# Split weight slots lengthened by 16 bytes, and the tokens of the four stages moved, in a two-layer fp32 decoder trunk

## The chip, the cores and the metric

The kernel runs on one core of one Trainium2 chip. The metric is the device time of one execution in microseconds (us). Before the change it is 2213.77 us, the median of two runs (2213.63 and 2213.91 us).

## What is computed

Two decoder layers over 256 tokens of 2048 features, all in float32. Layer 0 mixes tokens with sliding-window attention (mixer A: 32 query heads, 4 key/value heads, a sink and a position bias); layer 1 with forgetting attention (mixer B: 32 heads of queries, keys and values, decay sums in the logits). After each mixer, and after each gated MLP (up to 2 x 5632, a causal convolution of width 3, SiLU gate, down to 2048), stands a scaled residual and a layer norm:

```python
def conv_ffn(x, w_up, conv_w, conv_b, w_down):
    h = conv(x @ w_up, conv_w) + conv_b          # 2048 -> 2*5632, width 3, causal
    g, u = h[..., :D_FF], h[..., D_FF:]
    return (jax.nn.silu(g) * u) @ w_down

for i in range(DEPTH):                            # DEPTH = 2
    y = swa_sink_attention(x, ...) if i % 2 == 0 else forgetting_attention(x, ...)
    x = layer_norm(ALPHA * x + y, ln_g[i, 0], ln_b[i, 0])
    y = conv_ffn(x, ffn_w_up[i], ffn_conv_w[i], ffn_conv_b[i], ffn_w_down[i])
    x = layer_norm(ALPHA * x + y, ln_g[i, 1], ln_b[i, 1])
```

## The kernel before, in words

All weights are streamed once through SBUF, in chunks of 256 x 512 values (512 KB). Chunk after chunk lands in one of four slots of `raw` (SyncE issues the transfers, line 299). ScalarE rounds the chunk to the reduced float32r form in `w_hi` (line 478), VectorE writes the remainder to `w_lo` (line 757). The tokens are kept in the same way, as `xh` and `xl`. A product of two float32 values is then three float32r matmuls: low weights by high tokens, high weights by low tokens, high by high. TensorE takes chunks from the slots in turn (slot = chunk number mod 4), so that the slot changes each time two k-tiles of 128 rows have been used. Its order is fixed by the program; waits are on counting semaphores.

There are two forms of product. What a form streams through the array is the moving operand, and what is loaded first by a separate weight load is the stationary one.

- *Turned* (`turned_product`, lines 1189, 1191, 1192, and `turned_first`, line 1204): 128 columns of the weights are stationary, 256 tokens are moving. Used for the queries of A (768 matmuls), queries and keys of B (1536), and both up-projections (4224 each, 22 column groups x 16 k-tiles x 4 x 3). 10,752 matmuls in all.
- *Not turned* (`product`, lines 1171 to 1173): 128 tokens are stationary, 512 columns of the weights are moving. Used for the keys and values of A (96), the values of B (384), the output projections (2 x 384) and the down-projections (2 x 1056). 3360 matmuls in all. In the output projections the stationary operand is `oh` or `ol`, in the down-projections `hid_h` or `hid_l`, elsewhere `xh` or `xl`.

Between the matmuls of the products, TensorE does the transposes and the small matmuls of attention (lines 1318 to 1345).

Where things lie within a partition of SBUF: `raw`, `w_hi`, `w_lo`, `xh`, `xl`, `oh`, `ol`, `hid_h` and `hid_l` begin at multiples of 256 bytes; the fillers `fill_to_res` and `fill_to_xh` see to that. A slot of `w_hi` or `w_lo` is 2 x 512 values, 4096 bytes, so each of the four slots begins at a multiple of 256 bytes too. The tokens of the four stages (mixer A, MLP of layer 0, mixer B, MLP of layer 1) lie in the same `xh` and `xl`, but each stage begins at its own place in them, `PLACES`, counted in values of 4 bytes: 192, 32, 128 and 64 bytes from the start. A k-tile of tokens is 1024 bytes, and the part of a weight row that one weight load takes is 512 bytes, so the place modulo 256 bytes is the same for all matmuls of a stage.

```python
PLACES = (48, 8, 32, 16)
PLACED = D // P * SEQ + 64
w_hi = sb("w_hi", [P, RING, 2, COLS], F32R)
w_lo = sb("w_lo", [P, RING, 2, COLS], F32R)
xhs, xls = ([t[:, at:at + KT * SEQ].rearrange("p (k t) -> p k t", t=SEQ) for at in PLACES] for t in (xh_all, xl_all))
```

Of the kernel before, what the change touches and what calls it, by code (L numbers as in the profile page):

```python
# [22 lines left out]
F32R = mybir.dt.float32r  # L23
# [3 lines left out]
P = 128  # L27
# [2 lines left out]
MT = SEQ // P  # L30


PLACES = (48, 8, 32, 16)
PLACED = D // P * SEQ + 64
DEPTH = 2
HD = 64
# [5 lines left out]
COLS = 512  # L42
# [4 lines left out]
UP_PAIRS = D_FF // COLS  # L47
OUT_GROUPS = D // COLS
RING = 4
AHEAD = 3  # L50
LOW_AHEAD = 2
ALPHA = (2 * DEPTH) ** 0.25
# [75 lines left out]
def trunk(nc, x, a_w_qkv, a_w_o, a_sinks, rel_bias, b_w_qkvf, b_f_bias, b_w_o,  # L128
          ffn_w_up, ffn_conv_w, ffn_conv_b, ffn_w_down, ln_g, ln_b, out):
    ctx = ExitStack()  # L130
    with ctx:
        def sb(name, shape, dt=FP32, where=ctx):
            return where.enter_context(nc.sbuf_tensor(name, shape, dt))

        def sem(name):
            return ctx.enter_context(nc.semaphore(name))
# [13 lines left out]
        sb("fill_to_res", [P, (1920 - 1592) // 4])  # L150
        res = sb("res", [P, MT, D])
        raw = sb("raw", [P, RING, 2, COLS])
        w_hi = sb("w_hi", [P, RING, 2, COLS], F32R)
        w_lo = sb("w_lo", [P, RING, 2, COLS], F32R)
        tok = sb("tok", [P, MT, COLS])
        cg = sb("cg", [P, 4, SEQ])
        cu = sb("cu", [P, 4, SEQ])
        lnp = sb("lnp", [P, 2, COLS])
        convcol = sb("convcol", [P, DEPTH, 4, 2 * FT])
        sb("fill_to_xh", [P, 320])  # L160
        with ExitStack() as first:
            xh_all = sb("xh", [P, PLACED], F32R, first)
        with ExitStack() as later:
# [28 lines left out]
        hid_l = sb("hid_l", [P, FT, SEQ], F32R)  # L192
        xhs, xls = ([t[:, at:at + KT * SEQ].rearrange("p (k t) -> p k t", t=SEQ) for at in PLACES] for t in (xh_all, xl_all))
        ps = ctx.enter_context(nc.psum_tensor("ps", [P, 8, COLS], FP32))
# [6 lines left out]

        raw_in = [sem(f"raw_in{i}") for i in range(RING)]
        res_in = [sem(f"res_in{i}") for i in range(4)]
# [87 lines left out]
        def _(sp):  # L291
# [4 lines left out]
            def load_chunk(w, col, b4, loc, c):  # L296
                if not (isinstance(b4, int) and 4 * b4 + loc < RING):
                    sp.wait_ge(low_ready, b4 * 4 + (loc - RING + 1))
                sp.dma_start(raw[:, loc % RING], w[:, 2 * c:2 * c + 2, bass.ds(col, COLS)]).then_inc(raw_in[loc % RING], 16)
# [161 lines left out]
        def _(act):  # L461
# [9 lines left out]
            def split(b4, loc):  # L471

                if isinstance(b4, int) and 4 * b4 + loc >= CH_END:
                    return
                act.wait_ge(raw_in[loc % RING], b4 * 16 + 16 * (loc // RING + 1))
                if not (isinstance(b4, int) and 4 * b4 + loc < RING):
                    act.wait_ge(chunks_used, b4 * 4 + (loc - RING + 1))
                act.activation(w_hi[:, loc % RING], raw[:, loc % RING], ACT.Copy).then_inc(high_ready, 1)  # L478

            def slots(b4, loc0, nk=KT):  # L480

                for k in range(nk):
                    if k == nk - 2:
                        split(b4, loc0 + k // 2 + AHEAD)
                    yield k
                    if k % 2 == 0 and k != nk - 2:
                        split(b4, loc0 + k // 2 + AHEAD)

            def split_run(b4, loc0, count):

                while loc0 % 4 and count:
                    split(b4, loc0)
                    loc0, count = loc0 + 1, count - 1
                if count >= 8:
                    with act.Fori(0, count // 4) as i:
                        for c in range(4):
                            split(i + (b4 + loc0 // 4), c)
                    loc0, count = loc0 + count // 4 * 4, count % 4
                for c in range(count):
                    split(b4, loc0 + c)  # L500

            def xt_evacuate(xi, l, s, g):

                xh = xhs[xi]
                if xi == 0:
                    act.wait_ge(xt_turned, g + 1)
                    src = ps[:, X_BANK + g % 4, :].rearrange("p (a t) -> p a t", a=2)
                else:
                    if g == 0:
                        act.wait_ge(first_turned, xi)  # L510
                        act.activation(xh[:, 0, :], ps[:, FIRST_BANK, 0:SEQ], ACT.Identity,
                                       scale=lncol[:, 0, l, s, 0:1], bias=lncol[:, 1, l, s, 0:1]).then_inc(first_high, 1)
                        act.wait_ge(xt_turned, KC * xi + 1)
                        act.activation(xh[:, 1, :], ps[:, X_BANK, SEQ:2 * SEQ], ACT.Identity,
                                       scale=lncol[:, 0, l, s, 1:2], bias=lncol[:, 1, l, s, 1:2]).then_inc(xt_high, 1)
                        return
                    src = cg[:, 2 * (g % 2):2 * (g % 2) + 2, :]
                    if g in DVE_FULL:
                        act.wait_ge(xt_full, FULLS * (xi - 1) + DVE_FULL.index(g) + 1)
                    else:  # L520

                        act.wait_ge(xt_low, KC * xi + g - 1)
                        act.wait_ge(xt_turned, KC * xi + g + 1)
                        for a in range(2):
                            k = 2 * g + a
                            last = act.activation(cg[:, 2 * (g % 2) + a, :], ps[:, X_BANK + g % 4, a * SEQ:(a + 1) * SEQ],
                                                  ACT.Identity, scale=lncol[:, 0, l, s, k:k + 1], bias=lncol[:, 1, l, s, k:k + 1])
                        own.link(last)
                act.activation(xh[:, 2 * g:2 * g + 2, :], src, ACT.Copy).then_inc(xt_high, 1)
# [58 lines left out]
            def norm_and_first(xi, l, s):  # L588

                layer_norm(xi)  # L590
                act.wait_ge(norm_ready, xi)
                for i in range(2):
                    normalise(i)
                xt_evacuate(xi, l, s, 0)
                for i in range(2, 6):
                    normalise(i)
                xt_evacuate(xi, l, s, 1)
                for i in range(6, KC):
                    normalise(i)
# [80 lines left out]
            def up_finish(k, l, n):  # L680

                if k in (1, 3):
                    conv(cu, 1, l, n, k - 1, hid_low, n + l * UP_PAIRS)
                if k == 9:
                    act.wait_ge(prod_ready, n + (l * UP_PAIRS + 1))
                    act.activation(hid_h[:, bass.ds(n * 4, 4), :], cu[:, :, :], ACT.Copy).then_inc(hid_high, 1)

            def mlp(l):
# [18 lines left out]
                for k in slots(b4, 0, KT):  # L707
                    up_finish(k, l, UP_PAIRS - 1)
                split_run(b4, KC + AHEAD, OUT_GROUPS * FC - KC - (AHEAD if l == DEPTH - 1 else 0))

# [3 lines left out]
            xt_evacuate(0, 0, 0, 1)  # L714
            for c in range(1, AHEAD):
                split(0, c)
# [11 lines left out]
            for l in range(DEPTH):  # L728
                if l == 1:
                    mixer_b()  # L730

                split_run(CH_O[l] // 4, 2 * KC + AHEAD, (OUT_GROUPS - 2) * KC)
                norm_and_first(1 + 2 * l, l, 0)
# [778 lines left out]
```

## Time and profile before

| | |
|---|---|
| median of the two runs | 2213.77 us |
| the profiled execution, its own time | 2213.89 us |
| its span, first to last instruction | 2212.1 us |
| mean granted TensorE clock | 0.996 of full speed |
| TensorE matmul busy | 2182.2 us, 99% |
| VectorE, ScalarE, GpSimd busy | 60%, 47%, 10% |

1.8 us of the profiled execution lie outside its span. Matmuls are pipelined: a matmul of 256 columns is shown with some 280 ns, though the next one starts 113 to 120 ns later. So the shown duration of a matmul is no measure of its cost; what counts is the distance between the starts of two matmuls that follow each other. In the stretches 340 to 740 us (MLP of layer 0, up), 800 to 1000 us (its down-projection), 1500 to 1900 us (MLP of layer 1, up) and 1980 to 2180 us (its down-projection) TensorE does nothing but products.

### The profile page before, as it was taken

What the parts mean: (1) busy time and instruction counts of PE and PEld (TensorE: products, weight loads), DVE (VectorE), ACT (ScalarE), POOL (GpSimd) and SP (SyncE); (2) the same over time, 40 slices, a digit from 0 to 9 for tenths busy, and PEclk for the clock granted to TensorE, in tenths of its full rate; (3) what the DMA queues carried; (4) which work ended last, traced back from release to release, by engine and by line L of the source; (5) the groups of instructions that cost most, each with busy time, mean ns of one, the idle gap of its engine ahead of it and who ended that gap; (6) DMA issues with size and microseconds to landing.
All of it is one profiled execution on the core that took longest, in us unless ns stands there. A gap on an engine that the chain in (4) does not pass through costs nothing.

```text
span 2212.1 us, 40894 instructions
## 1 busy us (share of the span) xinstructions
PE 2182.2 (99%) x15265; PEld 2033.5 (92%) x15265; DVE 1335.3 (60%) x1805; ACT 1039.1 (47%) x1380; POOL 217.7 (10%) x206
## 2 busy tenths in 40 slices
PE   9999999999999999999999999999999999999996
PEld 7998899999999988888899998899999999988885
DVE  5565676666666555446665565576666566654455
ACT  4554464554555443335444444364545454543332
POOL 2000002210000000000340330002230000000001
PEclk9999999999999999999999999999999999999998
DMA  8544557666666666565655654656666666665563
GB/s 266 153 154 154 179 172 206 196 198 188 189 185 187 188 192 194 193 192 156 199 173 170 190 175 139 205 157 198 196 202 185 187 185 185 188 226 194 192 194 108
DMA packets 206952, 408.71 MB, mean 185 GB/s; under 512 B 12652, under 2 KB 13756, under 8 KB 206620
## 3 DMA queue, kind: packets, MB, share of 16 engines
q1 hardware_dynamic: 200192, 385.92, 57.2%
q0 software_dynamic: 5776, 21.34, 3.0%
q8 instruction: 49, 0.80, 0.2%
q10 hardware_dynamic: 908, 0.43, 0.1%
q14 instruction: 27, 0.22, 0.0%
HBM read 405.46 MB, written 2.18 MB: 184 GB/s over the span
## 4 chain that ended last, share of the span: by engine, by line
PE 96%; DVE 3%; ACT 0%; DMA 0%; issue 0%; SPq 0%; ACTq 0%; DVEq 0%
PE ps L1192 19%; PE ps L1189 19%; PE ps L1191 19%; PE ps L1171 11%; PE ps L1173 11%; PE ps L1172 11%; PE ps L1319 1%; PE ps L1326 1%; PE ps L1338 1%; PE ps L1337 1%; PE ps L1318 1%; PE ps L1336 0%; DMA raw<-in_a_w_qkv_dram 0%; DVE cg L803 0%; PE ps L1345 0%; PE ps L1268 0%
## 5 line engine op out<-in xcount | busy, mean ns | idle before, releaser
L757 DVE TENSOR_TENSOR w_lo<-raw,w_hi 128x1024 fp32r<-128x1024 f32 x728 | 923.6, 1274 | 652.4 <-ACT w_hi L478 651.9
L478 ACT ACTIVATE w_hi<-raw 128x1024 fp32r<-128x1024 f32 x728 | 771.2, 1060 | 974.2 <-PE ps L1192 557.6
L1189 PE MATMUL ps<-xh,w_lo 128*128 128x256 f32 x3572 | 1007.2, 282 | 2.2 <-DVE xl L799 1.6
L1192 PE MATMUL ps<-xh,w_hi 128*128 128x256 f32 x3572 | 999.0, 280 | 0.0
L1191 PE MATMUL ps<-xl,w_hi 128*128 128x256 f32 x3572 | 997.4, 279 | 0.0
L1189 PEld LDWEIGHTS ps<-xh,w_lo 128*128 128x128 f32 x3572 | 670.7, 188 | 5.2 <-DVE xl L799 3.0
L1191 PEld LDWEIGHTS ps<-xl,w_hi 128*128 128x128 f32 x3572 | 672.0, 188 | 0.4
L1192 PEld LDWEIGHTS ps<-xh,w_hi 128*128 128x128 f32 x3572 | 671.4, 188 | 0.0
L1171 PE MATMUL ps<-w_lo,hid_h 128*128 128x512 f32 x704 | 273.9, 389 | 0.0
L1173 PE MATMUL ps<-w_hi,hid_h 128*128 128x512 f32 x704 | 273.9, 389 | 0.0
L1172 PE MATMUL ps<-w_hi,hid_l 128*128 128x512 f32 x704 | 273.9, 389 | 0.0
L1173 PEld LDWEIGHTS ps<-w_hi,hid_h 128*128 128x128 f32 x704 | 132.2, 188 | 27.4
L1171 PEld LDWEIGHTS ps<-w_lo,hid_h 128*128 128x128 f32 x704 | 132.2, 188 | 27.4
L1172 PEld LDWEIGHTS ps<-w_hi,hid_l 128*128 128x128 f32 x704 | 132.2, 188 | 27.4
L400 POOL COPY cw<-convcol 128x16 f32 (+1 forms) x40 | 39.8, 994 | 779.3 <-DVE cu L1087 431.5
L1171 PE MATMUL ps<-w_lo,oh 128*128 128x512 f32 x256 | 102.4, 400 | 0.0
L1173 PE MATMUL ps<-w_hi,oh 128*128 128x512 f32 x256 | 99.9, 390 | 0.0
L1172 PE MATMUL ps<-w_hi,ol 128*128 128x512 f32 x256 | 99.7, 390 | 0.0
L1087 DVE SCALAR_TENSOR_TENSOR cu<-ps,cw,cu 128x254 f32<-128x254 f32 (+1 forms) x176 | 76.5, 476 | 1.6
L1087 DVE SCALAR_TENSOR_TENSOR cg<-ps,cw,cg 128x254 f32<-128x254 f32 (+1 forms) x176 | 76.5, 476 | 1.6
L1171 PE MATMUL ps<-w_lo,xh 128*128 128x512 f32 x160 | 64.2, 401 | 3.1 <-issue 2.6
L1173 PE MATMUL ps<-w_hi,xh 128*128 128x512 f32 x160 | 63.6, 398 | 0.0
(164 smaller groups left out, 1499.3 us busy)
## 6 DMA issues: line engine op xcount, KB each, us to landing
raw<-in_ffn_w_up_dram SPq DMA_DIRECT2D x352, 512.0 KB, 3.6
raw<-in_ffn_w_down_dram SPq DMA_DIRECT2D x176, 512.0 KB, 4.7
raw<-in_b_w_qkvf_dram SPq DMA_DIRECT2D x96, 512.0 KB, 4.4
raw<-in_a_w_qkv_dram SPq DMA_DIRECT2D x40, 512.0 KB, 4.5
raw<-in_a_w_o_dram SPq DMA_DIRECT2D x32, 512.0 KB, 4.6
raw<-in_b_w_o_dram SPq DMA_DIRECT2D x32, 512.0 KB, 4.7
bias<-rel_by_distance POOLq DMA_DIRECT2D x4, 1024.0 KB, 6.5
bias<-minus_cumulated_decay POOLq DMA_DIRECT2D x4, 1024.0 KB, 6.5
```

The costliest lines, as they stand in the source:

```text
L400: gp.tensor_copy(cw[:, h], convcol[:, l, :, bass.ds(n * 4 + h * FT, 4)]).then_inc(cw_ready, 1)
L478: act.activation(w_hi[:, loc % RING], raw[:, loc % RING], ACT.Copy).then_inc(high_ready, 1)
L757: dve.tensor_tensor(w_lo[:, s], raw[:, s], w_hi[:, s].bitcast(FP32), ALU.subtract).then_inc(low_ready, 1)
L1087: last = dve.scalar_tensor_tensor(dst[:, j, lag:SEQ], src, cw[:, h, tap, j:j + 1], dst[:, j, lag:SEQ], ALU.mult, ALU.add)
L1171: pe.matmul(o, lh[:, k, rows], w_lo[:, slot, k % 2, :], start=(k == 0), stop=False)
L1172: pe.matmul(o, ll[:, k, rows], w_hi[:, slot, k % 2, :], start=False, stop=False)
L1173: last = pe.matmul(o, lh[:, k, rows], w_hi[:, slot, k % 2, :], start=False, stop=(k == nk - 1))
L1189: pe.matmul(o, w_lo[:, slot, k % 2, cols], xh[:, k, :], start=(k == 0 and j % 2 == 0), stop=False, skip_group_check=True)
L1191: pe.matmul(o, w_hi[:, slot, k % 2, cols], xl[:, k, :], start=False, stop=False, skip_group_check=True)
L1192: last = pe.matmul(o, w_hi[:, slot, k % 2, cols], xh[:, k, :], start=False, stop=(k == KT - 1), skip_group_check=True)
L1318: pe.matmul(o[:, 0:P], qT[:, s // 2, 0:P], kz[:, kt, s % 2, 0:P], start=True, stop=True)
L1319: pe.matmul(o[:, P:SPAN], qT[:, s // 2, P:SEQ], kz[:, kt, s % 2, :], start=True, stop=True).then_inc(scores_ready, 1)
```

## The change

Each slot of `w_hi` and `w_lo` gets 4 values (16 bytes) more, which nothing uses. Slots 0 to 3 then begin 0, 16, 32 and 48 bytes past a multiple of 64 bytes (slot 0 of each tensor at a multiple of 256). A new filler lets `w_lo` begin at a multiple of 256 bytes again, and a shorter `fill_to_xh` leaves `xh` and all after it where they were; `tok`, `cg`, `cu`, `lnp` and `convcol` in between lie 320 bytes later. The tokens of the four stages move to 240, 192, 112 and 64 bytes. `raw` stays as it is. The instructions of each engine, their order and their waits stay the same.

```diff
-PLACES = (48, 8, 32, 16)
+PLACES = (60, 48, 28, 16)
 PLACED = D // P * SEQ + 64
...
 RING = 4
+SLOT = 2 * COLS + 4
...
-        w_hi = sb("w_hi", [P, RING, 2, COLS], F32R)
-        w_lo = sb("w_lo", [P, RING, 2, COLS], F32R)
+        w_hi = sb("w_hi", [P, RING, SLOT], F32R)[:, :, 0:2 * COLS].rearrange("p s (a c) -> p s a c", a=2)
+        sb("fill_to_w_lo", [P, 48])
+        w_lo = sb("w_lo", [P, RING, SLOT], F32R)[:, :, 0:2 * COLS].rearrange("p s (a c) -> p s a c", a=2)
...
-        sb("fill_to_xh", [P, 320])
+        sb("fill_to_xh", [P, 240])
```

## Rows read from the trace of the kernel before

**Rows 1.** The page: span, busy time of each engine, and the chain that ended last.

```profile
span 2212.1 us, 40894 instructions
PE 2182.2 (99%) x15265; PEld 2033.5 (92%) x15265; DVE 1335.3 (60%) x1805; ACT 1039.1 (47%) x1380; POOL 217.7 (10%) x206
...
PE 96%; DVE 3%; ACT 0%; DMA 0%; issue 0%; SPq 0%; ACTq 0%; DVEq 0%
```

**Rows 2.** Groups of instructions: busy us, mean ns of one, then idle time before, releaser.

```profile
L757 DVE TENSOR_TENSOR w_lo<-raw,w_hi 128x1024 fp32r<-128x1024 f32 x728 | 923.6, 1274 | 652.4 <-ACT w_hi L478 651.9
L478 ACT ACTIVATE w_hi<-raw 128x1024 fp32r<-128x1024 f32 x728 | 771.2, 1060 | 974.2 <-PE ps L1192 557.6
L1189 PE MATMUL ps<-xh,w_lo 128*128 128x256 f32 x3572 | 1007.2, 282 | 2.2 <-DVE xl L799 1.6
```

**Rows 3.** Timeline of TensorE, start us, us: layer 0, up-projection, 400 to 408 us.

```profile
399.74 0.28 PE L1191 MATMUL ps<-xl,w_hi 128*128 128x256 f32 x1
399.86 0.28 PE L1192 MATMUL ps<-xh,w_hi 128*128 128x256 f32 x1
...
407.91 0.28 PE L1192 MATMUL ps<-xh,w_hi 128*128 128x256 f32 x1
```

**Rows 4.** The same of layer 1, up-projection, 1600 to 1608 us.

```profile
1599.82 0.28 PE L1189 MATMUL ps<-xh,w_lo 128*128 128x256 f32 x1
...
1607.95 0.28 PE L1189 MATMUL ps<-xh,w_lo 128*128 128x256 f32 x1
```

**Rows 5.** The same of mixer B, queries and keys, 1064 to 1068 us.

```profile
1063.73 0.28 PE L1192 MATMUL ps<-xh,w_hi 128*128 128x256 f32 x1
...
1067.88 0.28 PE L1191 MATMUL ps<-xl,w_hi 128*128 128x256 f32 x1
```

**Rows 6.** The same of mixer A, queries, at 52 to 60 us and at 97 to 100 us.

```profile
51.80 0.28 PE L1192 MATMUL ps<-xh,w_hi 128*128 128x256 f32 x1
...
59.96 0.28 PE L1192 MATMUL ps<-xh,w_hi 128*128 128x256 f32 x1
...
96.81 0.28 PE L1191 MATMUL ps<-xl,w_hi 128*128 128x256 f32 x1
...
99.99 0.28 PE L1191 MATMUL ps<-xl,w_hi 128*128 128x256 f32 x1
```

**Rows 7.** The same of mixer B's 32-column weights, moving tokens as in rows 5.

```profile
1045.80 0.28 PE L1431 MATMUL ps<-xh,wf_hi 128*32 128x256 f32 x1
...
1050.00 0.28 PE L1429 MATMUL ps<-xh,wf_lo 128*32 128x256 f32 x1
```

**Rows 8.** The same of layer 1's first up-projection chunk, and the chunk after it.

```profile
1459.80 0.28 PE L1191 MATMUL ps<-xl,w_hi 128*128 128x256 f32 x1
...
1460.93 0.28 PE L1192 MATMUL ps<-xh,w_hi 128*128 128x256 f32 x1
...
1462.32 0.28 PE L1191 MATMUL ps<-xl,w_hi 128*128 128x256 f32 x1
...
1464.09 0.28 PE L1191 MATMUL ps<-xl,w_hi 128*128 128x256 f32 x1
```

**Rows 9.** The same of products not turned: mixer A, layer 0 down, mixer B.

```profile
27.70 0.39 PE L1171 MATMUL ps<-w_lo,xh 128*128 128x512 f32 x1
...
35.94 0.39 PE L1171 MATMUL ps<-w_lo,xh 128*128 128x512 f32 x1
...
849.63 0.39 PE L1171 MATMUL ps<-w_lo,hid_h 128*128 128x512 f32 x1
...
857.79 0.39 PE L1171 MATMUL ps<-w_lo,hid_h 128*128 128x512 f32 x1
...
1083.82 0.40 PE L1172 MATMUL ps<-w_hi,xl 128*128 128x512 f32 x1
...
1091.99 0.39 PE L1171 MATMUL ps<-w_lo,xh 128*128 128x512 f32 x1
```

**Rows 10.** Windows of TensorE: us, busy (instructions), granted clock, DMA share, GB/s.

```profile
340.00:740.00 400.00, 400.00 (x3431) 1.00 0.66 192
1500.00:1900.00 400.00, 400.00 (x3398) 1.00 0.65 191
800.00:1000.00 200.00, 200.00 (x884) 1.00 0.61 193
1980.00:2180.00 200.00, 200.00 (x884) 1.00 0.59 190
```

## The prediction, made before the changed kernel was run

> **What bounds the kernel now.** I read the page first. The chain that ended last lies on TensorE for 96% of the span, and its matmuls are busy for 99% [rows 1]. So nothing that changes only VectorE or ScalarE can matter unless it makes TensorE late. Then the groups, to see who waits for whom: the rounding on ScalarE (1060 ns a chunk) and the subtraction on VectorE (1274 ns a chunk) run 728 times; ScalarE stands idle 974 us ahead of its roundings, most of it until a matmul gives the slot free, and the main group of TensorE lost 2.2 us in waits [rows 2]. The weights are ready ahead of time. There is nothing to gain from waits: the time is the number of matmuls times the distance from one start to the next. That distance the groups do not show (they give 282 ns, with overlap), so the third view is the timeline, and the distance is last start minus first start over the number of steps between.
>
> For the turned form (256 moving tokens, 128 stationary weight columns):
> - MLP of layer 0, tokens at 32 bytes: (407.91 - 399.74) / 70 = 116.7 ns, 71 rows [rows 3].
> - MLP of layer 1, tokens at 64 bytes: (1607.95 - 1599.82) / 69 = 117.8 ns, 70 rows [rows 4].
> - Mixer B, at 128 bytes: (1067.88 - 1063.73) / 35 = 118.6 ns, 36 rows [rows 5].
> - Mixer A, at 192 bytes: (59.96 - 51.80) / 72 = 113.3 ns over 73 rows, and later in the same stage, between the same kinds of operand at the same places, (99.99 - 96.81) / 27 = 117.8 ns over 28 rows [rows 6].
>
> The windows confirm that the two MLP figures hold throughout, not just in the samples: 3431 matmuls in 400 us against 3398, the granted clock 1.00 in both [rows 10]. Same instructions, same clock, same neighbours; the place of the tokens is what differs by construction. So places do cost time, about 1% between two stages.
>
> What is the floor? In mixer B, 48 matmuls stream the same tokens at 128 bytes but load only 32 columns of weights: (1050.00 - 1045.80) / 37 = 113.5 ns, 38 rows [rows 7]. With the tokens at their worst place, the small weight load takes the whole excess away. I read this as two terms: about 113.3 ns that 256 moving columns cost in any case, and an excess of 0 to 5 ns that appears when a full weight load runs beside the stream and meets it badly. Mixer A has both conditions at one place, so the meeting depends on the phase between the two as well, and it stays as it falls: layer 1's MLP ran its first chunk at (1460.93 - 1459.80) / 10 = 113 ns, and after a wait and four transposes at (1464.09 - 1462.32) / 15 = 118 ns, and has stayed there [rows 8].
>
> For the form not turned (512 moving weight columns, 128 stationary tokens): 226.7 ns in the down-projection, both operands at multiples of 256 bytes, (857.79 - 849.63) / 36; 228.9 ns in mixer A, stationary tokens at 192, that is 64 short of 256, (35.94 - 27.70) / 36; 233.4 ns in mixer B, tokens at 128, (1091.99 - 1083.82) / 35 [rows 9]. 226.7 is twice 113.3: this form is at its floor where it is used most.
>
> **How much can be had at all.** The excess over the floor: layer 0 up 4224 x 3.4 = 14.4 us; layer 1 up 4224 x 4.5 = 19.0; mixer B 1536 x 5.3 = 8.1; mixer A 768 x 2.2 (half of it in each condition) = 1.7; the values of B 384 x 6.7 = 2.6. In sum 45.8 us, 2.1% of the time. The change moves no instruction and adds no wait; all it can do is gain from these 45.8 us or add to the distances.
>
> **The change part by part.** Two things move: the tokens, and three of four weight slots, which now begin 16, 32 and 48 bytes off a 64-byte boundary. So within a stage the distance between the two operands changes each time the slot changes, after 24 turned matmuls, where now it is the same throughout.
>
> Layer 0 up, tokens at 192: the place of mixer A, where 113.3 and 117.8 both occur. Bounds per matmul: 113.3 (a slot change frees the phase and it stays good) and 118.6 (the worst place seen). With a new phase in each slot I take the middle of the two conditions, 115.5: 4224 x -1.2 = -5.1 us (-14.4 to +8.0).
>
> Layer 1 up, tokens unchanged at 64: both conditions occurred there too [rows 4, 8]. Now it is stuck in the bad one; slots at four distances keep moving it. Again 115.5: 4224 x -2.3 = -9.7 us (-19.0 to +3.4).
>
> Mixer B, queries and keys, tokens from 128 to 112: distances to the slots are 112, 96, 80 and 64. No row has them. Between 113.3 and 120 (its worst steps are about 1.5 above its mean, an estimate); I take the 116.7 of the only place off a 64-byte boundary [rows 3]: 1536 x -1.9 = -2.9 us (-8.1 to +2.2). Its values: halfway from 233.4 to the floor, 384 x -3.4 = -1.3 us (-2.6 to +2.6).
>
> Mixer A, from 192 to 240: 0 us (-1.7 to +3.4), 768 matmuls in two conditions already.
>
> The form not turned in the down- and output projections is the price. 2880 matmuls, now at the floor, stream weights that begin off the boundary in three slots of four. No row shows a moving weight row off it. The nearest is the 2.3 ns that a distance of 64 bytes costs in mixer A [rows 9]; in proportion 16, 32 and 48 bytes give 0.6, 1.1 and 1.7 ns, with slot 0 a mean of 0.9: 2880 x 0.9 = +2.5 us. Bounds: 0, and mixer B's 6.7 ns on three quarters of them, +14.5 us.
>
> The roundings and subtractions write and read the moved slots. At 1060 and 1274 ns against 2800 ns of products a chunk (24 x 116.7) they stay hidden even if each became half as long again; 0 us. The tensors between `w_lo` and `xh` lie 320 bytes later: off the path, 0 us.
>
> Sum: -5.1 - 9.7 - 2.9 - 1.3 + 0 + 2.5 = -16.5 us. Against the profiled execution's own 2213.89 us, which stands 0.1 above the median, that is 2197.4 us.
>
> Here a rule of the Trainium skill speaks against the change. The page "TensorE: Matmul & The Clock Gate" (section "Step-by-step: what each phase is for") says that TensorE has two independent read ports on SBUF, one for the streamed operand and one for the weight load, so that loading the next weights takes no read bandwidth from the running matmul. By it no placement matters and the sum is 0. The trace does not agree here: 113.5 ns with 32 columns loaded against 118.6 ns with 128, at the same tokens [rows 5, 7].
>
> **The rivals.**
> - *No effect, about 2213.8 us.* The excess belongs to the stage (what was before it, its mix of neighbours), not to distances, and one stretch at 117 is replaced by another. For it: mixer A ran at 113.3 and 117.8 with the same places, so place alone decides nothing. Against it: two MLPs with the same program keep 116.7 and 117.8 for hundreds of microseconds each [rows 3, 4, 10].
> - *Slower, about 2229 us.* The start of an operand off a 64-byte boundary costs one piece more. If the stream goes in pieces of 16 columns (64 bytes), one is 113.3 / 16 = 7.1 ns. Place: down- and output projections, slots 1 to 3: 2160 x 7.1 = +15.3 us; weight loads that begin off the boundary read one more piece too and meet the stream as often as now, so the turned form gains nothing. It decides from 8.8 ns a matmul if the turned form gains what I forecast (19.0 / 2160), and from any price at all if it gains nothing. For it: no matmul that streams weights off a boundary has been seen. Against it: the tokens at 32 bytes are off it too and their 3.4 ns of excess is the lowest of the steady stages.
> - *Nearly the whole pool, about 2175 us.* Every slot change lets the stream settle at 113.3 and the other form stays at 226.7: 45.8 us less, of which some 39 are realistic with the disturbances of attention. For it: 113.3 exists at two of the places [rows 6, 8]. Against it: nothing shows the good condition holding after a disturbance.
> - That the change doesn't do what it says: a slot at 4112 bytes is a plain layout, and neither engine's instruction changes form. I give it nothing of its own.
>
> **How the numbers follow.** Chances: forecast 0.48, slower 0.25, no effect 0.17, nearly the whole pool 0.10. The likeliest gives 2197. Its own range, from half to one and a half times the gains and prices, is 2186 to 2208. To leave out no more than 2 in 10 the range reaches past the slower case and most of the way to the full pool: 2175 to 2231. A change of 2% (44.3 us, about what a measurement of this kernel can tell from no change) needs the whole pool of 45.8 us on the fast side, 0.02; on the slow side every price at its upper bound (8.0 + 3.4 + 2.2 + 2.6 + 3.4 + 14.5 = 34.1 us) does not reach it, 0.02 for what I have not thought of. Within 2%: 0.96.
>
> **What would show it.** In the timeline of the changed kernel the up-projections should show different distances in different slots, changing every 24 matmuls, with a mean near 115.5 ns; 3464 instead of 3431 and 3398 matmuls in windows of 400 us. The down-projection should show 226.7 ns in slot 0 and up to 2 ns more in the others, so 880 or more in 200 us instead of 884. Mixer B should fall to some 117 ns. I am wrong if the up-projections keep one distance through all slots (place beside slot then has no part), if they exceed 117.8, or if the down-projection falls under 865 in 200 us, which is the slower case.

## The result and the profile after

The changed kernel takes 2232.55 us (two runs, 2232.53 and 2232.57) against 2213.77 us before: a ratio of 1.0084, 95% interval 1.0068 to 1.0101. It is 18.8 us slower, where I had forecast 16.5 us faster; the range of 2175 to 2231 us ends 1.6 us short of it.

The page after the change: span, busy time, and the chain that ended last.

```profile
span 2230.8 us, 40894 instructions
PE 2200.8 (99%) x15265; PEld 2038.9 (91%) x15265; DVE 1337.8 (60%) x1805; ACT 1040.1 (47%) x1380; POOL 215.9 (10%) x206
...
PE 96%; DVE 3%; ACT 0%; issue 0%; DMA 0%; DVEq 0%; ACTq 0%
...
L759 DVE TENSOR_TENSOR w_lo<-raw,w_hi 128x1024 fp32r<-128x1024 f32 x728 | 926.2, 1278 | 665.6 <-ACT w_hi L480 665.0
L480 ACT ACTIVATE w_hi<-raw 128x1024 fp32r<-128x1024 f32 x728 | 772.1, 1061 | 992.5 <-PE ps L1194 561.5
L1191 PE MATMUL ps<-xh,w_lo 128*128 128x256 f32 x3572 | 1009.4, 283 | 2.3 <-DVE xl L801 1.6
```

Set beside [rows 1, 2]: the number of instructions is the same, the rounding and the subtraction take 1061 and 1278 ns as before, and TensorE's waits are 2.3 against 2.2 us. Nothing waits for anything new; the span has grown by 18.7 us and TensorE's busy time by 18.6. ScalarE's idle time grew by 18.3 us: it stands waiting for TensorE a little longer. (Lines are two further down than before: 1191, 1193, 1194 are the turned form, 1173 to 1175 the form not turned.)

Windows of TensorE in the changed kernel, columns as in [rows 10]:

```profile
340.00:740.00 400.00, 400.00 (x3405) 1.00 0.65 191
1500.00:1900.00 400.00, 400.00 (x3400) 1.00 0.66 191
800.00:1000.00 200.00, 200.00 (x863) 1.00 0.59 188
1980.00:2180.00 200.00, 200.00 (x863) 1.00 0.59 189
```

Against 3431, 3398, 884 and 884. Layer 0's up-projection got slower, layer 1's hardly moved, and both down-projections got through 2.4% fewer matmuls in the same time at the same clock. Where the 18.8 us come from, by the first and last starts of each stage's matmuls in the two timelines: down-projections 239.18 to 244.83 us and 239.16 to 244.84 us, together +11.3; output projections +3.4; layer 0 up 497.09 to 500.95, +3.9; layer 1 up 501.66 to 501.42, -0.2; mixer A +2.0; mixer B -1.6.

The step from one start to the next, averaged by slot over a stage (distances between neighbouring matmuls of the product, waits left out):

| ns | slot 0 | slot 1 | slot 2 | slot 3 | mean | before |
|---|---|---|---|---|---|---|
| layer 0, up | 114.3 | 118.8 | 117.3 | 120.0 | 117.6 | 116.7 |
| layer 1, up | 117.9 | 116.6 | 116.7 | 119.7 | 117.7 | 117.8 |
| down (both) | 230.4 | 231.5 | 233.7 | 232.7 | 232.1 | 226.7 |

So the steps do differ from slot to slot, as forecast, but the down-projection is slow even in slot 0, where both operands begin at a multiple of 256 bytes as before (slot 0 of `w_hi` in the same place, that of `w_lo` 256 bytes later). These 863 matmuls in 200 us are also under the 865 that the prediction named as the sign of its slower case. The timeline of the changed kernel (start us, us) through slot 0 of one chunk, the first and last rows of its 12 matmuls, and the first of the next slot:

```profile
858.98 0.39 PE L1173 MATMUL ps<-w_lo,hid_h 128*128 128x512 f32 x1
859.21 0.39 PE L1174 MATMUL ps<-w_hi,hid_l 128*128 128x512 f32 x1
859.44 0.40 PE L1175 MATMUL ps<-w_hi,hid_h 128*128 128x512 f32 x1
...
861.29 0.39 PE L1174 MATMUL ps<-w_hi,hid_l 128*128 128x512 f32 x1
861.52 0.39 PE L1175 MATMUL ps<-w_hi,hid_h 128*128 128x512 f32 x1
861.75 0.39 PE L1173 MATMUL ps<-w_lo,hid_h 128*128 128x512 f32 x1
```

(861.75 - 858.98) / 12 = 230.8 ns, where [rows 9] had 226.7.

### The profile page after: what moved, and what is told of

It reads as the page before. It is cut to its first block, busy times and chain, and to the rows that moved or that the text cites. A ratio compares the mean times of both kernels' runs of the same rounds, so it can differ in the third digit from the quotient of the medians.

```text
span 2230.8 us, 40894 instructions
## 1 busy us (share of the span) xinstructions
PE 2200.8 (99%) x15265; PEld 2038.9 (91%) x15265; DVE 1337.8 (60%) x1805; ACT 1040.1 (47%) x1380; POOL 215.9 (10%) x206
## 4 chain that ended last, share of the span: by engine, by line
PE 96%; DVE 3%; ACT 0%; issue 0%; DMA 0%; DVEq 0%; ACTq 0%
PE ps L1191 19%; PE ps L1193 19%; PE ps L1194 19%; PE ps L1173 12%; PE ps L1175 12%; PE ps L1174 12%; PE ps L1321 1%; PE ps L1328 1%; PE ps L1340 1%; PE ps L1339 1%; PE ps L1320 1%; PE ps L1338 0%; PE ps L1270 0%; DVE cg L805 0%; PE ps L1347 0%
## 5 line engine op out<-in xcount | busy, mean ns | idle before, releaser
L759 DVE TENSOR_TENSOR w_lo<-raw,w_hi 128x1024 fp32r<-128x1024 f32 x728 | 926.2, 1278 | 665.6 <-ACT w_hi L480 665.0
L480 ACT ACTIVATE w_hi<-raw 128x1024 fp32r<-128x1024 f32 x728 | 772.1, 1061 | 992.5 <-PE ps L1194 561.5
L1174 PE MATMUL ps<-w_hi,xl 128*128 128x512 f32 x160 | 63.6, 397 | 0.0
```

Source lines behind the costliest of these rows:

```text
L759: dve.tensor_tensor(w_lo[:, s], raw[:, s], w_hi[:, s].bitcast(FP32), ALU.subtract).then_inc(low_ready, 1)
L1174: pe.matmul(o, ll[:, k, rows], w_hi[:, slot, k % 2, :], start=False, stop=False)
```

## The experiments

Places are given here modulo 256 bytes, as in the description of the kernel. In some of the edits below a tensor that is lengthened pushes the next one (`w_lo`, `ol`, `hid_l`) a further multiple of 256 bytes along; I take that to be without effect, which no run shows by itself.

Three theories stood at the start: the distance between the two operands of a matmul sets the step; the start off a 64-byte boundary does; or the change of distance from slot to slot does. In what follows "up 0" and "up 1" are the up-projections of the two layers.

### First batch: the two halves of the change, and the slots laid out in other ways

**Slots lengthened, tokens left.** (`w_lo` here and below has the same edit as `w_hi` unless it is shown, and the filler behind them is shortened so that `xh` stays.)

```diff
-        w_hi = sb("w_hi", [P, RING, 2, COLS], F32R)
+        w_hi = sb("w_hi", [P, 4160], F32R)[:, 0:4112].rearrange("p (s r) -> p s r", s=RING)[:, :, 0:2 * COLS].rearrange("p s (a c) -> p s a c", a=2)
```

> Slots of the split weights lengthened by 16 bytes as in the change, tokens left at 192, 32, 128 and 64 bytes. Theory D (the distance between the two operands modulo some bytes sets the step, in both forms, so the slots are the cause): down-projections at 232.1 ns a matmul as after the change, output projections 232, about +16 us from the form not turned; time 2228 to 2234 us. Theory P (the new places of the tokens are the cause of a good part): under 2222 us. The up-projection of layer 1 has the same tokens as after the change and should repeat its 117.9, 116.6, 116.7 and 119.7 ns in slots 0 to 3.

Measured 2240.68 us (2240.45 to 2240.83), ratio 1.0121, 1.0104 to 1.0138. Down-projections 230.3, 231.5, 233.7 and 232.7 ns in slots 0 to 3, up 1 at 117.9, 116.6, 116.7 and 119.6: the changed kernel's numbers, though the tokens lie elsewhere in all stages but the last. The total is over what I had expected because up 0, tokens at 32 bytes, rose to a mean of 118.9 ns. So the slots alone cost 26.9 us, and beside them the new places bring 8.1 us back.

The same run answers a reading of the prediction. The 48 matmuls of mixer B that load only 32 columns of weights have their tokens and their weights (`wf_hi`, `wf_lo`) exactly where they lay before, and use no slot. Before they took 113.5 ns [rows 7]. Here, as start us and us:

```profile
1063.93 0.28 PE L1429 MATMUL ps<-xh,wf_lo 128*32 128x256 f32 x1
1064.05 0.28 PE L1430 MATMUL ps<-xl,wf_hi 128*32 128x256 f32 x1
...
1068.97 0.28 PE L1429 MATMUL ps<-xh,wf_lo 128*32 128x256 f32 x1
```

(1068.97 - 1063.93) / 42 = 120.0 ns, as slow as any steady step of the turned form, with the small weight load beside it. The kernel with all slots at 16 bytes shows 120.0 ns there too; those with slots 64 bytes apart, at 32 or at 48 bytes show 113.6. Same matmuls, same places, two steps. What differs for TensorE is the slots that the matmuls ahead of them used; a small weight load does not take the excess away.

**Tokens moved, slots left.**

```diff
-PLACES = (48, 8, 32, 16)
+PLACES = (60, 48, 28, 16)
```

> Tokens moved to 240, 192, 112 and 64 bytes as in the change, slots left at 4096 bytes. Both theories: the down-projections stay at 226.7 ns. Theory D (distance): the up-projection of layer 0 at one distance throughout, either 113.3 or 117.8 ns, the two that mixer A showed at this place, so -14 or +5 us; layer 1 unchanged at 117.8; time between 2198 and 2220 us. Theory P (the places carry the loss): over 2222 us.

Measured: ten executions in two groups, four at 2195.5 to 2195.8 us and six at 2213.9 to 2214.2. The gap of 18.4 us is 4224 x 4.4 ns, one up-projection between 117.7 and 113.3 ns. The profile is of a long execution: up 0 at 117.7, up 1 at 117.8, down at 226.7, mixer B down from 118.8 to about 114 ns. At 192 bytes both conditions do occur, and which of them a whole up-projection runs in is decided anew in each execution. (That the short ones have up 0 at 113.3 is inferred from the gap, and from up 1 having the slots and tokens of before, whose executions show one group; none of the short ones was profiled.)

**All slots 16 bytes off, and slots 64 bytes apart.** Both keep to before's tokens.

```diff
-        w_hi = sb("w_hi", [P, RING, 2, COLS], F32R)
+        w_hi = sb("w_hi", [P, 4160], F32R)[:, 4:4100].rearrange("p (s r) -> p s r", s=RING)[:, :, 0:2 * COLS].rearrange("p s (a c) -> p s a c", a=2)
```

```diff
-        w_hi = sb("w_hi", [P, RING, 2, COLS], F32R)
+        w_hi = sb("w_hi", [P, 4160], F32R)[:, 0:4160].rearrange("p (s r) -> p s r", s=RING)[:, :, 0:2 * COLS].rearrange("p s (a c) -> p s a c", a=2)
```

> All slots begin 16 bytes past a multiple of 256 bytes, 4096 bytes apart; tokens as before. Theory H (what costs is that the distance changes from slot to slot, so that the stream is disturbed each time): down-projections back at 226.7 ns, time near 2214 us. Theory B (the start of the moving weights off a 64-byte boundary costs by itself): 231 to 234 ns in all slots, about +14 us from the form not turned, 2228 us or more.

> Slots 4160 bytes apart, so that they begin 0, 64, 128 and 192 bytes past a multiple of 256; tokens as before. Theory B (boundary of 64 bytes): nothing is off it, down-projections at 226.7 ns, time near 2214 us. Theory H (changing distance costs) and theory D modulo 256 bytes: down-projections 229 to 233 ns in at least three slots, as mixers A and B had with stationary tokens at 192 and 128 bytes, +8 to +16 us.

All at 16 bytes: 2229.7 us in two executions and 2240.9 in two; the profile is of a short one, with the down-projections at 231.7 ns in every slot. No distance changes there, and 5.0 of the 5.4 ns are lost all the same: that the changes between slots carry the loss falls. Slots 64 bytes apart: 2236.74 us, down-projections at 228.4, 230.3, 232.9 and 232.9 ns. Neither operand of the down-projection is off a 64-byte boundary there: that this boundary carries it falls too. That left the distance.

### Second batch: is it the distance?

```diff
-PLACES = (48, 8, 32, 16)
+PLACES = (52, 12, 36, 20)
...
-        w_hi = sb("w_hi", [P, RING, 2, COLS], F32R)
+        w_hi = sb("w_hi", [P, 4160], F32R)[:, 4:4100].rearrange("p (s r) -> p s r", s=RING)[:, :, 0:2 * COLS].rearrange("p s (a c) -> p s a c", a=2)
...
+            oh, ol = (sb(name, [P, KT * SEQ + 128], F32R, mix)[:, 4:4 + KT * SEQ].rearrange("p (k t) -> p k t", t=SEQ) for name in ("oh", "ol"))
...
+        hid_h, hid_l = (sb(name, [P, FT * SEQ + 128], F32R)[:, 4:4 + FT * SEQ].rearrange("p (k t) -> p k t", t=SEQ) for name in ("hid_h", "hid_l"))
```

> Every operand of the products moved by 16 bytes: slots at 16 past a multiple of 256, tokens of the stages at 208, 48, 144 and 80, oh, ol, hid_h and hid_l at 16. All distances are those of the kernel before, all absolute starts are not. Theory D (only the distance between the two operands counts): down-projections back at 226.7 ns, up-projections at 116.7 and 117.8, time 2214 us. Theory A (an operand's own start off a boundary costs): down-projections stay at 231.7 ns as with the slots alone at 16 bytes, +11 us or more.

> The kernel with every operand moved by 16 bytes once more, for a profile of another execution: six of its ten executions took 2215.5 us, four 2238.7 us, and the profile is of a long one. If this one is short, its down-projections show 226.7 ns and its up-projections 116.7 and 117.8 (the same places, another condition of the stream). If short executions get their time from elsewhere, the down-projections stay at 231 to 233 ns.

Ten executions in two groups, 2215.4 to 2215.8 and 2238.6 to 2238.9 us. The shorter group stands 1.6 us above the 2213.97 us that before took beside it, and by the total alone I would have taken the distance for proven. The second profile is of an execution of 2215.13 us. Windows of TensorE in it (up 0, up 1, down 0, down 1):

```profile
340.00:740.00 400.00, 400.00 (x3383) 1.00 0.65 189
1500.00:1900.00 400.00, 400.00 (x3532) 1.00 0.68 199
800.00:1000.00 200.00, 200.00 (x867) 1.00 0.59 189
1980.00:2180.00 200.00, 200.00 (x867) 1.00 0.59 187
```

The down-projections are not back: 867 in 200 us, 231.1 ns. Up 0 is slower than before (118.3 ns), and up 1 runs at the floor (3532 in 400 us, 113.4 ns). Two losses and a gain happen to add up to before's time. With every distance (modulo 256 bytes) as before the steps are others: the distance alone does not decide either. In the long execution of the same kernel the windows for up 1 and the down-projections read:

```profile
1500.00:1900.00 400.00, 400.00 (x3382) 1.00 0.66 190
800.00:1000.00 200.00, 200.00 (x867) 1.00 0.60 189
1980.00:2180.00 200.00, 200.00 (x859) 1.00 0.60 192
```

Same places, 118.3 instead of 113.4 ns, and two down-projections of one execution at 231.1 and 233.3. By first and last starts up 1 is 20.7 us longer than in the short execution and down 1 2.3 us, which is the gap of 23.2 us.

The slots at 32 and at 48 bytes, tokens as before, differ from the kernel with all slots at 16 bytes in two numbers:

```diff
-        w_hi = sb("w_hi", [P, 4160], F32R)[:, 4:4100]
+        w_hi = sb("w_hi", [P, 4160], F32R)[:, 8:4104]
```

```diff
-        w_hi = sb("w_hi", [P, 4160], F32R)[:, 4:4100]
+        w_hi = sb("w_hi", [P, 4160], F32R)[:, 12:4108]
```

> All slots 32 bytes past a multiple of 256, 4096 bytes apart, tokens as before. Distance theory: down-projections in all slots what slot 2 of the changed kernel shows, 233.8 ns, since there the distance is 32 too. If the changed distance from slot to slot carried the loss, it would be 226.7 to 229 ns.

> All slots 48 bytes past a multiple of 256, tokens as before. Distance theory: down-projections at slot 3's 232.7 ns in all slots. Then only slot 0's 230.3 ns in the changed kernel, at distance 0, is left to the changes between slots.

2245.98 and 2250.01 us. Down-projections at 233.3 ns in all slots of both, near what slots 2 and 3 of the changed kernel show (233.7 and 232.7), but not equal to it. With the kernels before that gives, for each place of the slots alone, the step it has when nothing changes from slot to slot:

| ns | slots at 0 | 16 | 32 | 48 bytes | mean of the four | lengthened slots |
|---|---|---|---|---|---|---|
| down | 226.7 | 231.7 | 233.3 | 233.3 | 231.3 | 232.1 |
| up 0, tokens at 32 | 116.7 | 117.4 | 120.0 | 118.3 | 118.1 | 118.9 |
| up 1, tokens at 64 | 117.8 | 116.7 | 116.7 | 120.0 | 117.8 | 117.7 |

The lengthened slots (last column: the kernel with slots lengthened and tokens left) give the mean of their four places, and up to 0.8 ns on top. The down-projection's 5.4 ns are 4.6 for the places and 0.8 for the changes. Each number is of one profiled execution. That matters for up 0 at 16 bytes: the two long executions of that kernel stand 11.2 us above the profiled one, as one up-projection at 120.0 instead of 117.4 ns would (not shown, they have no profile). With 120.0 the mean of up 0 would be 118.8, and next to nothing would be left for the changes there.

The table also shows that a place is good or bad only beside another: slots at 32 instead of 0 bytes cost up 0 3.3 ns a matmul and give up 1 1.1 ns back.

**Tokens of all stages at 112 bytes.**

```diff
-PLACES = (48, 8, 32, 16)
+PLACES = (28, 28, 28, 28)
```

> Slots as before, tokens of all four stages at 112 bytes, the place at which mixer B came down from 118.8 to 114 ns. Theory D (distance alone sets the step of the turned form): both up-projections at 113.3 to 115 ns, -10 to -32 us, time 2182 to 2204 us; mixer A's queries near 114. Theory F (the condition that a stage falls into depends on how it starts, whatever the place): the up-projections stay at 116 to 118 ns or differ between executions, 2200 to 2215 us.

> Tokens of all stages at 112 bytes, slots as before, once more in more executions. If the condition at 113.4 ns is a matter of the place, all executions take 2175.8 to 2176.4 us. If it is one of two, as at 192 bytes, some take 2194 us or more, one up-projection back at 117.8 ns.

2175.85 us (four executions, 2175.77 to 2176.36; ratio 0.9827, 0.9811 to 0.9844), and again 2175.79 us (five executions, 2175.59 to 2176.15; ratio 0.9828, 0.9814 to 0.9841). All nine agree: here one condition holds. The page and the windows of the first of the two kernels:

```profile
span 2174.1 us, 40894 instructions
PE 2144.0 (99%) x15265; PEld 1994.2 (92%) x15265; DVE 1330.6 (61%) x1805; ACT 1039.7 (48%) x1380; POOL 222.1 (10%) x206
```

```profile
340.00:740.00 400.00, 400.00 (x3532) 1.00 0.68 197
1500.00:1900.00 400.00, 400.00 (x3532) 1.00 0.68 197
800.00:1000.00 200.00, 200.00 (x884) 1.00 0.61 193
```

And the timeline of up 1, to be read beside [rows 4]:

```profile
1599.81 0.28 PE L1192 MATMUL ps<-xh,w_hi 128*128 128x256 f32 x1
...
1607.97 0.28 PE L1192 MATMUL ps<-xh,w_hi 128*128 128x256 f32 x1
```

73 rows: (1607.97 - 1599.81) / 72 = 113.3 ns, through all slots. The up-projections take 483.3 us each, 13.8 and 18.4 us less than before, and mixer B 5.9 us less. This is the version that beats both kernels: 38.1 us, 1.7%, by one line of four numbers. It also speaks against the distance alone: here slots at 0 and tokens at 112 bytes give mixer B's queries and keys 114.3 ns; slots at 16 and tokens at 128, the same 112 apart, gave them 119.5 (the kernel with all slots at 16 bytes).

### Third batch: which part, and what the neighbours do

Tokens at 112 bytes and lengthened slots:

```diff
-PLACES = (48, 8, 32, 16)
+PLACES = (28, 28, 28, 28)
...
-        w_hi = sb("w_hi", [P, RING, 2, COLS], F32R)
+        w_hi = sb("w_hi", [P, 4160], F32R)[:, 0:4112].rearrange("p (s r) -> p s r", s=RING)[:, :, 0:2 * COLS].rearrange("p s (a c) -> p s a c", a=2)
```

> Tokens of all stages at 112 bytes, and the slots lengthened by 16 bytes as in the change. Only the slots differ from the kernel with all tokens at 112 bytes (2175.9 us). If each slot has its own step, as mixer B showed after the change at the same tokens (about 115.5, 119.5, 119.7 and 117.8 ns in slots 0 to 3): up-projections at a mean of 118.1 ns, +40 us; down- and output projections at 232, +15 us; time about 2232 us. If the tokens' place alone made the up-projections fast: 113.4 ns kept, time about 2191 us.

2238.52 us, 62.7 us above the same tokens with before's slots. The up-projections have 115.4, 119.6, 119.9 and 118.4 ns in slots 0 to 3 and the down-projections 230.4, 231.5, 233.8 and 232.7. So the slots spoil the good place, and it is here that they cost most.

Only the slots of `w_lo` 16 bytes later:

```diff
-        w_lo = sb("w_lo", [P, RING, 2, COLS], F32R)
+        w_lo = sb("w_lo", [P, 4160], F32R)[:, 4:4100].rearrange("p (s r) -> p s r", s=RING)[:, :, 0:2 * COLS].rearrange("p s (a c) -> p s a c", a=2)
```

> Only the slots of w_lo begin 16 bytes past a multiple of 256; those of w_hi and all tokens as before. Distance theory: of the three matmuls of a product in the down-projection only the one that streams w_lo is at a distance of 16, so a third of the loss of all slots at 16 bytes: a mean of 228.3 ns. A disturbance of the whole sequence would give 231.7 ns again.

2234.48 us; down-projections at 232.0 ns, not 228.3. One matmul in three streams from a moved place, and the sequence of three loses as much as with all of them moved. The step is a property of the sequence, not of the single matmul. (Up 0 went from 116.7 to 117.8 ns here, up 1 stayed at 117.8.)

```diff
-PLACES = (48, 8, 32, 16)
+PLACES = (24, 20, 36, 40)
```

> Slots as before, tokens of the four stages at 96, 80, 144 and 160 bytes. Distance theory from uniform slots: mixer A (96) near 119.8 ns, layer 0 up (80) near 118.1, mixer B (144) near 119.4, layer 1 up (160) near 118.3. If 112 bytes is one of a range of good places, 96 or 80 give 113 to 115 ns. The down-projections stay at 226.7 ns.

2228.38 us: 119.7 ns at 96 bytes (mixer A), 118.3 at 80 (up 0), 118.8 at 144 (mixer B), 118.6 at 160 (up 1), down at 226.7. I had 119.8, 118.1, 119.4 and 118.3 from other absolute places at the same distance. The numbers are near, but all of these are bad places, between 118 and 120, so this says little for the distance. It does say that 112 is a narrow place: 16 bytes below it mixer A's step is 119.7 ns, at 112 bytes it is 114.8.

The stationary operands of the output and down-projections alone 16 bytes later:

```diff
+            oh, ol = (sb(name, [P, KT * SEQ + 128], F32R, mix)[:, 4:4 + KT * SEQ].rearrange("p (k t) -> p k t", t=SEQ) for name in ("oh", "ol"))
...
+        hid_h, hid_l = (sb(name, [P, FT * SEQ + 128], F32R)[:, 4:4 + FT * SEQ].rearrange("p (k t) -> p k t", t=SEQ) for name in ("hid_h", "hid_l"))
```

> Only oh, ol, hid_h and hid_l begin 16 bytes past a multiple of 256; slots and tokens as before. If the moving weights' own start is what costs, the down-projections stay at 226.7 ns, 2214 us. If it is the pair of places, they go up to 229 to 233 ns, +6 to +17 us, though the moving operand is where it was.

2232.0 us. The up-projections stay at 116.7 and 117.8 ns, and the down-projections go to 233.3 with the moving operand where it was. Windows of the two down-projections:

```profile
800.00:1000.00 200.00, 200.00 (x859) 1.00 0.59 188
1980.00:2180.00 200.00, 200.00 (x858) 1.00 0.59 188
```

So the moving operand's own start is not all that costs: one of the two operands moved, whichever, costs 5.0 or 6.6 ns, and both moved by the same cost 4.4 to 6.6. By these numbers alone each operand's start off its old place could cost by itself. That the pair counts is shown by the up-projections in the table above, where the same move of the slots slows one stage and speeds up the other.

Slots 0 and 2 in their old alignment, 1 and 3 16 bytes off it:

```diff
+class Slots:
+    STARTS = (0, 1028, 2112, 3140)
+    def __init__(self, t):
+        self.slots = [t[:, at:at + 2 * COLS].rearrange("p (a c) -> p a c", a=2) for at in self.STARTS]
...
+        w_hi, w_lo = (Slots(sb(name, [P, 4224], F32R)) for name in ("w_hi", "w_lo"))
```

> Slots 0 and 2 begin at a multiple of 256 bytes, slots 1 and 3 16 bytes past one; tokens as before. If a slot's step is its own, the down-projections show 226.7 ns in slots 0 and 2 and 231.7 in 1 and 3, mean 229.2. If a chunk pays for the slot before it, slots 0 and 2 lie at 229 to 231 ns, as slot 0 of the changed kernel (230.3), and the mean at 230.5 or more.

2229.65 us. Down-projections at 229.1, 231.5, 229.1 and 231.4 ns. Slots 0 and 2 are aligned as before, beside stationary operands that lie where they did, and pay 2.4 ns each for the slot ahead of them. (Up 1 alternates between 117.7 and 116.7 ns, its steps at 0 and 16 bytes in the table, to 0.1; up 0 between 116.8 and 119.5.) The timeline (start us, us) through slot 0, 12 matmuls and the first of the next slot, shows how:

```profile
904.02 0.39 PE L1181 MATMUL ps<-w_lo,hid_h 128*128 128x512 f32 x1
...
905.18 0.39 PE L1183 MATMUL ps<-w_hi,hid_h 128*128 128x512 f32 x1
905.41 0.39 PE L1181 MATMUL ps<-w_lo,hid_h 128*128 128x512 f32 x1
905.64 0.39 PE L1182 MATMUL ps<-w_hi,hid_l 128*128 128x512 f32 x1
...
906.77 0.39 PE L1181 MATMUL ps<-w_lo,hid_h 128*128 128x512 f32 x1
```

The first six steps take (905.41 - 904.02) / 6 = 231.7 ns, the next six (906.77 - 905.41) / 6 = 226.7. The stream needs half the chunk to find back into its good condition, and then the slot changes again. In the changed kernel slot 0 has slot 3 ahead of it and finds back only in its last two steps.

## Why the prediction was wrong

**What held.** The time is the number of matmuls times the step; no wait, no VectorE or ScalarE work came into it; the steps differ by slot and change every 24 turned matmuls; 113.3 and 226.7 ns are the floors (no stage of any kernel had a mean under them); and the pool of 45.8 us was real, since the kernel with all tokens at 112 bytes took 38.1 of them. The rule of the Trainium skill on two read ports ("TensorE: Matmul & The Clock Gate", section "Step-by-step: what each phase is for") was read in the prediction as saying that no placement matters. That consequence is contradicted by the changed kernel and by most of the others.

**The step that failed first: the price of the form not turned.** I put it at 0.9 ns by proportion from the 2.3 ns (2.2 by its rows) that a distance of 64 bytes costs in mixer A. Measured is 5.4 ns in the down-projections, and +14.7 us with the output projections (+11.3 + 3.4) where I had +2.5. The proportion was the error. The slot tables show a jump, not a slope: 226.7 at 0, 231.7 at 16, 233.3 at 32. The upper bound that I had set aside, mixer B's 6.7 ns on three quarters of the matmuls, gave +14.5, within 0.2 us of the measured price. That close it is luck: the bound left slot 0 free, which lost 3.7 ns, and gave 6.7 to the others, which lost 5.9 on average. But it was the slowest row of the same form, and there was no reason in the trace to prefer the other.

**The second: the middle of two conditions for the up-projections.** I took 115.5 ns, as if each slot drew between 113.3 and 117.8. But those are the two conditions of one pair of places. The other pairs have steps of their own, 116.7 to 120.0 in the uniform kernels, and three of four slots are such pairs. Layer 1: forecast -9.7, measured -0.2; its mean is that of four uniform kernels, 117.7 against 117.8 ns, so its places account for it. Layer 0: forecast -5.1, measured +3.9, with slot 0 at 114.3, the gain that I had hoped for, and the other three at 118.7 on average. Mixer B: -4.2 with its values, measured -1.6. Mixer A: 0, measured +2.0.

In sum: 12.2 us from the first step, 18.5 from the up-projections, 2.6 and 2.0 from the mixers make 35.3, the distance between -16.5 and +18.8.

**A reading beside the sum that did not hold.** The prediction took the excess for something that only a full weight load brings, from 113.5 ns with 32 columns loaded against 118.6 with 128 [rows 5, 7], and set that against the rule of the Trainium skill. With 32 columns loaded and nothing moved the same matmuls took 120.0 ns in two other kernels, so that comparison shows neither a part of the load's size nor whether load and stream share a port.

**The rivals.** The slower one named the right place, and its 2229 us are 3.6 us off, but its mechanism is not borne out: a piece more for a start off a 64-byte boundary would spare slots 64 bytes apart (they lose 4.4 ns) and would not touch a kernel in which only the stationary operand moves (it loses 6.6). What I had against it, that tokens at 32 bytes ran best, was an argument against the boundary and not against the loss. "No effect" was off by 18.8 us, though the fact that it rested on, one place with two steps, came back in three kernels whose executions fall into two groups. "Nearly the whole pool" failed for this change (slot changes do not free the stream), but its 2175 us are what the tokens at 112 bytes give without any slot moved.

**What stays open.** By what rule a pair of places gives its step. Neither the distance, nor the boundary of 64 bytes, nor one operand alone explains the tables. That the weight load and the stream disturb each other through the memory they both read is my guess; every matmul here has a weight load beside it, so no run separates the two reads. What the other engines do at a moment does not change the step: in up 0 of the kernel before the step is 116.7 ns where VectorE and ScalarE are both at work (1092 steps) and where both are idle (397 steps), and 116.7 ns both with no DMA packet under way (607 steps) and with 14 or more (1959 steps). Nor is it shown what decides, from execution to execution, between the two conditions at some pairs.

## What to carry to other kernels

When TensorE never waits and yet takes longer a matmul than in another stage of the same shape, read the start-to-start step by stage and by buffer slot, and try the starts of both operands, one number at a time: here one line was worth 38 us. Let every slot of a ring have the same alignment: here a ring whose slots differed got the mean of good and bad places, and in the down-projection paid at each change besides. And judge a layout by the steps of each stage in several executions, not by the total: two wrong conditions and a right one gave before's time to 2 us.

## What the runs showed of the hardware that I had not expected

- The step jumps with 16 bytes of placement: down-projection 226.7 to 233.3 ns for moving `hid_h` and `hid_l` by 16 bytes; turned form of mixer A 114.8 ns at 112 bytes and 119.7 at 96, of mixer B 114.3 at 112 and 118.8 at 128.
- Moving only the slots of `w_lo` costs the whole sequence as much (232.0 ns) as moving all slots (231.7).
- The same 48 matmuls with 32 columns loaded, at the same places, take 113.6 or 120.0 ns a step, in kernels that differ in the slots used before them.
- After a disturbance the good condition comes back by itself at one pair (six steps in the down-projection at 0 and 0), while at others the slower one holds for nearly all of a stage's 4224 matmuls (up 1 of the long execution with everything moved by 16 bytes, 118.3 ns; its short one holds 113.4).
- One program with the same data has executions 18.4 us apart (tokens at 240, 192, 112, 64), 11.1 us (slots at 16) or 23.2 us (everything at 16), in two sharp groups; the kernel before and the one with tokens at 112 show one group each.
